# Differential attention: in heads 1 to 3 the query rows come long and short in alternation instead of in rising order

## The reference, cut to what matters

```
s = einsum('bqhcd,bkhcd->bhcqk', qblk, k) * scale      # c = 0, 1: two maps
p = softmax(where(kpos <= qpos, s, NEG), axis=-1)
a = p[:, :, 0] - lam * p[:, :, 1]
o = einsum('bhqk,bkhd->bqhd', a, v)
```

## Time and profile before

| | |
|---|---|
| median of 3 runs | 2450.82 us (2450.37 to 2453.84) |
| the profiled execution | 2448.42 us, span 2446.7 us, mean granted clock of TensorE 0.936 |
| differential attention: first L583 to last L533 | 510.51 to 889.47 us of the span |
| TensorE, VectorE, ScalarE, GpSimd over the span | 86%, 55%, 46%, 18% busy |

### The profile page before, as it was taken

One profiled execution on the slowest core, in us unless ns is written; L12 is line 12 of the kernel. 1 busy time (PEld: TensorE's weight loads), 2 busy tenths in 40 slices (PEclk: granted clock), 3 DMA queues, 4 the chain that ended last, 5 costly groups with the idle time before them and its releaser, 6 DMA issues. The chain is left out here.

```text
span 2446.7 us, 39746 instructions
## 1 busy us (share of the span) xinstructions
PE 2094.9 (86%) x12636; PEld 1763.1 (72%) x12637; DVE 1344.9 (55%) x2175; ACT 1114.4 (46%) x2340; POOL 428.4 (18%) x568
## 2 busy tenths in 40 slices
PE   3999999969999956969998278999999999999940
PEld 2888888747777746967887267888887887788840
DVE  4232333268888844643332767665467466655537
ACT  3111111158877844642222157555456456645512
POOL 0111211124344333001111300000000000000036
PEclk9999999969999988989999589999999999999975
DMA  5233333241244456332332379777679679877648
GB/s 194 85 92 104 91 102 96 83 142 53 80 128 125 134 137 151 93 93 81 113 114 71 108 241 342 267 271 258 224 266 317 215 263 320 279 244 257 214 149 298
DMA packets 324203, 421.85 MB, mean 172 GB/s; under 512 B 19616, under 2 KB 236320, under 8 KB 324128
## 3 DMA queue, kind: packets, MB, share of 16 engines
q1 hardware_dynamic: 303696, 349.80, 45.1%
q0 software_dynamic: 12672, 46.14, 5.7%
q10 hardware_dynamic: 7760, 24.97, 2.5%
HBM read 321.76 MB, written 99.09 MB: 172 GB/s over the span
## 5 line engine op out<-in xcount | busy, mean ns | idle before, releaser
L56 PE MATMUL proj<-w_in_lo,n1T_hi 128*128 128x512 f32 (+1 forms) x640 | 244.2, 382 | 2.4 <-DVE n1T_lo L257 2.4
L58 PE MATMUL proj<-w_in_hi,n1T_hi 128*128 128x512 f32 (+1 forms) x640 | 239.1, 374 | 0.0
L57 PE MATMUL proj<-w_in_hi,n1T_lo 128*128 128x512 f32 (+1 forms) x640 | 239.1, 374 | 0.0
L509 ACT ACTIVATE prob<-score,nmax 128x512 f32<-128x512 f32 (+3 forms) x344 | 206.7, 608 | 51.5 <-DVE nmax L583 47.2
L1678 DVE TENSOR_TENSOR wg_lo<-raw_pieces,wg_hi 128x1024 fp32r<-128x1024 f32 x124 | 146.9, 1222 | 120.4 <-ACT wg_hi L1646 120.3
L58 PE MATMUL u_ps<-wu_hi,xT_hi 128*128 128x256 f32 x752 | 211.4, 281 | 0.0
L57 PE MATMUL u_ps<-wu_hi,xT_lo 128*128 128x256 f32 x752 | 211.4, 281 | 0.0
L56 PE MATMUL u_ps<-wu_lo,xT_hi 128*128 128x256 f32 x752 | 211.2, 281 | 0.0
L545 POOL TENSOR_SCALAR prob<-prob,scale,lam 128x512 f32<-128x512 f32 (+3 forms) x172 | 147.8, 870 | 242.0 <-DVE scale L599 225.7
L583 DVE TENSOR_REDUCE nmax<-score 128x2 f32<-128x1024 f32 (+3 forms) x172 | 171.7, 998 | 28.3 <-PE score L623 19.5
L56 PE MATMUL y_ps<-wd_lo,hT_hi 128*128 128x512 f32 x376 | 157.1, 418 | 29.4 <-DVE hT_lo L1689 29.0
(11 more groups left out here) (234 smaller groups left out, 4979.9 us busy)
## 6 DMA issues: line engine op xcount, KB each, us to landing
raw_pieces<-in_w_gate SPq DMA_DIRECT2D x128, 512.0 KB, 5.9
raw_pieces<-in_w_up SPq DMA_DIRECT2D x128, 512.0 KB, 6.9
raw_pieces<-in_w_down SPq DMA_DIRECT2D x128, 512.0 KB, 4.7
qk_scratch<-qkT SPq DMA_DIRECT2D x96, 256.0 KB, 2.3
y_scratch<-y ACTq DMA_DIRECT2D x47, 512.0 KB, 6.7
x_sb<-in_x SPq DMA_DIRECT2D x32, 512.0 KB, 4.4
y_scratch<-zero SPq DMA_DIRECT2D x32, 512.0 KB, 4.0
w_in_raw<-in_w_in SPq DMA_DIRECT2D x9, 1024.0 KB, 5.2
```

The source lines that it names most:

```text
L56: pe.matmul(out, hi, w_lo, start=first, stop=False)
L57: pe.matmul(out, lo, w_hi, start=False, stop=False)
L58: return pe.matmul(out, hi, w_hi, start=False, stop=last)
L509: act.activation(prob[:, n % RING, c, 0:w], score[:, n % BUFS, c, 0:w], ACT.Exp, bias=nmax[:, c, n:n + 1], accum_out=part[:, c, n:n + 1]). ...
```

## The change

Head 0 keeps its rising order. In heads 1 to 3 the rows are 15, 1, 14, 2, 13, 3, 12, 4, 11, 5, 10, 6, 9, 7, 8, 0. Before, head 3 ran 1 to 15 and then 0. Steps are cut as before, and no instruction is added or taken away but waits. Since row 15, the first of a head, needs all four chunks, `NEEDS` now is a list for each step, and the first step of heads 1 to 3 waits for four chunks. The loads of the next head are therefore issued at the rows with the places 0, 4, 8, 12 of head 0, and 0, 3, 6, 9 of heads 1 and 2.

```diff
-    ORDER = [(h, i) for h in range(DIFF_HEADS - 1) for i in range(TILES)]
-    ORDER += [(DIFF_HEADS - 1, i) for i in range(1, TILES)] + [(DIFF_HEADS - 1, 0)]
+    ORDER = [(0, i) for i in range(TILES)]
+    for h in range(1, DIFF_HEADS):
+        for far, near in zip(range(TILES - 1, TILES // 2 - 1, -1), [*range(1, TILES // 2), 0]):
+            ORDER += [(h, far), (h, near)]
...
+    PLACES = [(0, 4, 8, 12), (0, 3, 6, 9), (0, 3, 6, 9)]
...
-    NEEDS = {min(n for n in range(N) if STEPS[n][0] == h and STEPS[n][1] * P // CHUNK >= c): (h, c)
-             for h in range(DIFF_HEADS) for c in range(CHUNKS)}
+    NEEDS = [[c for c in range(CHUNKS) if n == min(u for u in range(N) if STEPS[u][0] == STEPS[n][0]
+                                                   and STEPS[u][1] * P // CHUNK >= c)] for n in range(N)]
...
-                    if h + 1 < DIFF_HEADS and (i + 1) * P % CHUNK == 0:
-                        load(h + 1, i * P // CHUNK)
+                    place = m % TILES
+                    if h + 1 < DIFF_HEADS and place in PLACES[h]:
+                        load(h + 1, PLACES[h].index(place))
...
-                        if n in NEEDS:
-                            pe.wait_ge(chunk_in[NEEDS[n][1]], (h + 1) * LOAD)
+                        for chunk in NEEDS[n]:
+                            pe.wait_ge(chunk_in[chunk], (h + 1) * LOAD)
```

## The result

| | before | after |
|---|---|---|
| median of 11 runs each | 2450.82 us (2446.94 to 2456.49) | 2461.84 us (2457.19 to 2467.40) |
| the profiled execution | 2448.42, span 2446.7 | 2457.19, span 2455.4 |
| the stage: first maximum to last row copy | 510.51 to 889.47: 378.96 us | 509.74 to 898.50: 388.76 us |

The ratio is 1.0039, with a 95% interval of 1.0028 to 1.0051: the changed kernel is slower by 9.6 us by this ratio, by 11.0 us between the medians, where 3.3 us faster was forecast. The time lies outside the range given (2438 to 2458). In the two profiled executions the stage is longer by 9.80 us and the whole span by 8.7, so the whole loss is in the stage.

A forecast was written before the change was run, and what follows sets the result against it. TensorE and VectorE were taken to bound the kernel in two regimes within each head. Terms 3 x (-1.1 + 0.75), +2.1, -3.0 and -1.3 gave -3.3 us, a median of 2447.5, range 2438 to 2458.

The forecast's parts named there:

- The pairs of a long and a near short row: First four pairs of heads 1 to 3: 50.4 us against 51.54 before, a gain of 1.1 us a head.
- second rival: VectorE's three slow slots lie together in a pair and stop TensorE: slower by +2 to +11 us, chance 0.28.
- the second group: Pairs 11 with 5, 10 with 6, 9 with 7, 8 with 0: 42.4 us against 41.65, losing 0.75 a head.
- the walk: Slot-by-slot tracing of engine waits through a long-short pair: 1.6 of 14.2 us absorbed, so 12.6 us a pair.
- The other pairs: Last four pairs of a head, 19 slots: 42.4 us against 41.65, a loss of 0.75 us a head.
- The start of head 1: Long steps now lie over head 0's long steps, making TensorE's scores dearer in seven slots: +2.1 us.
- The end of the stage: After the last maximum: two 512-key steps fewer behind GpSimd and a smaller rest, -3.0 us.
- Head 3: Head 3 up to its last maximum: 90.85 us against 92.49 before, a further -1.3 us.
- The loads: Four chunks needed at once at head 1's start: landing 1.8 us before needed, costed at nothing.
- The rule on interleaving regimes: Within each head, TensorE's and VectorE's regimes alternate; interleaving them may improve performance, which spoke for the change; no size.
- first rival: Full interleaving in heads 1 to 3: -20 us, 2431 median; more interleaving than forecast (-6 to -20) had chance 0.25.

The follow-up runs named there:

- the one kernel profiled twice: Changed order with one more slot between scores and turning and the row copy ahead of the exponentials, against the kernel before: median 2433.27 us, ratio 0.9935.

## Why the prediction was wrong

**The pairs of a long and a near short row** is the step that failed. I took 12.6 us each and 50.4 for four; they took 13.98, 13.44, 13.34 and 13.87, together 54.63, a loss of 3.1 us a head in place of a gain of 1.1. The sums were right: both engines could do a pair in under 12, and all of it turned on the slack that I got by walking. In that walk TensorE turned the long row's first step and went on to its product at once. But the product has to wait until the short row has been copied out, behind the exponential of the long step. I named this very wait for the second group, and left it out here, where it is longest (1.40 us). In head 2 TensorE's own waits for the copy (PE, as in the waits above) grew from 2.60 us to 7.22, 4.27 of them in the first four pairs. With the copy ahead of the exponentials the pair 14|2 takes 12.93 and not 13.44, which is nearer the walk; four pairs still take 53.0. The walk also had a combination at 0.66 us from start to start in the slot where the next long row begins, and there it takes 1.03 (723.13 to 724.16). With the copy moved and GpSimd's work halved, four pairs take 51.16, near the 50.4 of the walk.

The time itself came out as in the case that I had as second rival, at a chance of 0.28: it went from +2 to +11 us, and my range cut it off at +7. Its mechanism, VectorE's three slow slots lying together, put the pair at up to 13.5; the average is 13.66, and the copy's wait is no part of it. It is shown in one part, GpSimd's scaling: 0.47 us less in VectorE's slow slots shortened the pair 14|2 by 0.48. That this wait is as long in the profile after as in that before (17.6 and 17.9 us) says nothing of its cost: before, it fell into a slot beside long steps, where TensorE had scores and products of full length to do; after, into a short slot, between two sets of statistics. The experiments show that it costs more there; this reading of why is argued from the order of the slots.

**The other pairs**: 42.4 forecast, 42.81 measured: near, a loss of 1.16 us a head for 0.75. TensorE's waits for the copy do grow there, as I said: in head 2 from none in the second half to 2.95 us in the last nineteen slots.

**The start of head 1**: +2.1 forecast, +0.28 measured: head 1 lost 4.53 us and head 2, which has no such start, 4.25. I priced full slots in place of short ones, with nothing to hide in. But the first pair takes 14.45 us in head 1, over the long rows that end head 0, and 13.98 in head 2, over the shorter rows 8 and 0. Why so little more, no run shows.

**The end of the stage**: -3.0 forecast, -2.05 measured. Two long steps fewer were right, but the two short ones that replace them don't come free: the last turnings start at 894.64, 896.12 and 897.12, since the last two each stand behind the product of a long step in TensorE's queue.

```profile
894.64 0.63 PE L640 MATMUL aT_ps<-ident,prob 128*128 128x128 f32 x4
...
896.12 0.27 PE L640 MATMUL aT_ps<-ident,prob 128*128 128x128 f32 x1
...
897.12 0.27 PE L640 MATMUL aT_ps<-ident,prob 128*128 128x128 f32 x1
...
898.50 0.27 ACT L537 COPY o_diff<-o_ps 128x128 f32<-128x128 f32 x1 [0.58 <-PE o_ps L650]
```

**Head 3** up to its last maximum: 90.85 forecast, 95.39 measured, which is head 2 less the 2.02 us of row 0's slot, as reckoned, on the wrong base.

**The loads**: no wait of TensorE for a DMA at the start of head 1, and nothing in the experiment with the loads alone. Right.

**The rule on interleaving regimes.** The Trainium skill, "Perfetto Trace Analysis", section "Optimization Strategy", says that interleaving regimes may improve performance, and so it spoke for a gain. Here the two regimes were mixed, and the kernel lost 4.25 us in head 2; when most of the waits for the copy and for GpSimd were taken out, mixing won nothing (89.17 against 88.90 us). My first rival, built on it, was as wrong as the forecast.

What stays open: the remaining 0.27 to 0.45 us a head, and how GpSimd's part divides into its answer and what it slows in VectorE beside it: I only halved its work, and taking it away wasn't tried. Nor was a second PSUM tile for the row's output, which might end the copy's wait at its root.

## What to carry to other kernels

When engines run in lockstep through slots, write out for one period what each slot waits for *on every engine*, and check each single-buffered tile there: the sum of work says only what is possible. A reordering makes a period; compare it with the pipeline's depth, because at equality the same coincidence comes back in every period. Here both were six, and with a lag of seven the order cost 0.45 us in head 2 instead of 4.25; no other period was tried. And before reordering work to hide a wait, see if the waited-for instruction stands behind something that it doesn't need: moving the row copy ahead of two exponentials was worth 2.2 us a head in the old order and 4.5 in the new, as much as the order of the rows cost.

## What the runs showed of the hardware

TensorE's clock moves head 0, whose order of rows is the same everywhere, by more than many of the differences above. The window 512 to 524 us of the kernel before (not among the rows above), of the order before with GpSimd's work halved, and of the changed order with GpSimd's work halved:

```profile
512.00:524.00 12.00, 11.76 (x63) 7.93 (x62) 9.84 (x33) 8.83 (x41) 3.59 (x7) 0.50 0.49 162
```

```profile
512.00:524.00 12.00, 10.32 (x71) 7.06 (x68) 10.86 (x38) 9.63 (x42) 3.11 (x7) 0.74 0.46 151
```

```profile
512.00:524.00 12.00, 11.69 (x67) 8.02 (x67) 9.32 (x35) 9.43 (x44) 2.91 (x7) 0.50 0.63 210
```

The engine had been nearly idle before (busy 2.76 of the 12 us up to 512 in the kernel before), and was busy most of the time from there on. In the second execution the granted clock rose from its lower level, 1.2 GHz, to 2.4 GHz halfway through the window; in the other two it stayed at the lower level to the window's end. Rows 2 to 5 took 14.16, 12.73 and 14.41 us. GpSimd's shorter instructions aren't the reason, since the third has them too, and needs 1.7 us more for these rows than the second. Nor is it the kernel: in the one kernel profiled twice the window's clock was 0.50 once and 0.66 the other time. What sets the moment, no run shows. For a change of a few microseconds this means that the stretch behind an idle time of TensorE is not the place to measure in.

The second thing is VectorE beside GpSimd. A combination of 512 keys took 1.12 us in the changed order where the same one took 0.76 with GpSimd's scaling halved. But most combinations that overlap with GpSimd's scaling take 0.75 all the same, and no run isolates when one is slowed.
